# Product-key expert slots worked in chunks of two instead of four, with a head's routing split into five pieces

## What is computed

```python
def peer_ffn(xn, w_query, sub_keys, peer_u, peer_v):
    q = (xt @ w_query).reshape(t, PEER_HEADS, 2, PEER_HALF)
    sk = jnp.einsum('thcd,ckd->thck', q, sub_keys).astype(jnp.float32)
    top_s, top_i = lax.top_k(sk, PEER_TOPK)
    cand_s = top_s[:, :, 0, :, None] + top_s[:, :, 1, None, :]
    ...
    best_s, best_pos = lax.top_k(cand_s, PEER_TOPK)
    idx = jnp.take_along_axis(cand_i, best_pos, axis=-1)
    gate = jax.nn.softmax(best_s, axis=-1)
    ...
        h = jnp.einsum('thkd,td->thk', peer_u[ib], xb).astype(jnp.float32)
        a = (gb * jax.nn.gelu(h, approximate=False)).astype(xb.dtype)
        return jnp.einsum('thk,thkd->td', a, peer_v[ib])
```

## Time and profile before

| | |
|---|---|
| median of 3 runs | 3038.73 us (3035.6 to 3039.03) |
| profiled execution | 3042.86 us, span 3041.1 us |
| busy: PE, DVE, ACT, POOL | 69%, 71%, 37%, 39% of the span |
| share of DMA in the chain that ended last | 37% |
| bytes moved | 1170.89 MB, of which 1073.81 MB are gathers |

### The profile page before, as it was taken

The page is one execution under the profiler, slowest core; times in us unless marked ns, Lnnn a source line. Parts: engine busy times, 40 slices in busy tenths (PEclk is TensorE's granted clock), DMA queues, the critical chain, the costliest instruction groups (busy, mean ns, idle before and its releaser), DMA issues.

```text
span 3041.1 us, 37523 instructions
## 1 busy us (share of the span) xinstructions
PE 2109.0 (69%) x12704; PEld 1048.0 (34%) x12704; DVE 2148.6 (71%) x5267; ACT 1129.8 (37%) x3444; POOL 1191.1 (39%) x1028
## 2 busy tenths in 40 slices
PE   7868688667886877566676777667677556565556
PEld 6654354224442433133343343224344111111111
DVE  4645678887667778777656878887766777776665
ACT  3412345653233444533223445552323322222222
POOL 0014333343443344343444444343444444444443
PEclk9889899778987898788888889878998767767777
DMA  4159999989999999999999999989999999999998
GB/s 158 61 219 418 375 410 414 385 342 414 404 419 406 416 419 419 370 351 419 413 410 420 415 396 420 401 355 392 420 420 421 418 420 419 419 417 419 409 421 357
DMA packets 173840, 1170.89 MB, mean 385 GB/s; under 512 B 19280, under 2 KB 19408, under 8 KB 42576
## 3 DMA queue, kind: packets, MB, share of 16 engines
q0 software_dynamic: 147456, 1073.81, 86.2%
q1 hardware_dynamic: 26192, 94.68, 8.1%
HBM read 1166.32 MB, written 2.10 MB: 384 GB/s over the span
## 4 chain that ended last, share of the span: by engine, by line
DMA 37%; DVE 23%; PE 23%; ACT 8%; issue 6%; POOL 3%; DVEq 0%; SPq 0%; POOLq 0%; ACTq 0%
DMA gather<-experts,idx 37%; PE ysum L548 13%; DVE gather L1039 12%; PE bank L406 5%; POOL gather L364 3%; DVE sd L816 3%; PE bank L507 2%; ACT diag L755 2%; ACT amp L747 2%; ACT L597 1%; ACT gel L740 1%; DVE x L1016 1%; ACT sd L597 1%; DVE shared L843 0%; PE bank L453 0%
## 5 line engine op out<-in xcount | busy, mean ns | idle before, releaser
L364 POOL DMA_INDIRECT gather<-experts,idx x1024 | 1190.9, 1163 | 1830.1 <-PE ysum L548 1492.2
L548 PE MATMUL ysum<-gather,diag 64*64 64x512 f32 x8192 | 1277.6, 777 | 797.3 <-ACT diag L755 751.2
L1039 DVE CUSTOM_DVE_ANT_0 gather<-gather,xc 128x1024 f32<-128x1024 f32 x1024 | 1224.3, 1224 | 585.8 <-DMA gather<-experts,idx 583.5
L548 PEld LDWEIGHTS ysum<-gather,diag 64*64 64x64 f32 x8192 | 369.6, 174 | 1606.4 <-ACT diag L755 966.9
L740 ACT ACTIVATE gel<-hdot 128x4 f32<-128x4 f32 x255 | 52.4, 205 | 1662.9 <-DVE hdot L1039 1662.9
L406 PE MATMUL bank<-xnT,w 128*128 128x256 f32 x1984 | 468.9, 392 | 11.8 <-DVE xnT L805 11.8
L406 PEld LDWEIGHTS bank<-xnT,w 128*128 128x128 f32 x1984 | 378.3, 195 | 108.8 <-issue 45.3
L755 ACT ACTIVATE diag<-cc,amp 128x64 f32<-128x64 f32 x1020 | 268.5, 333 | 2.2 <-PE ysum L548 2.2
L747 ACT ACTIVATE amp<-gel,gate 128x1 f32<-128x1 f32 x1020 | 216.8, 283 | 8.3
L816 DVE RECIPROCAL sd<-sd 128x256 f32<-128x256 f32 x60 | 105.1, 1751 | 119.5 <-ACT sd L597 119.3
L740 ACT ACT_TABLE_LOAD x124 | 159.1, 1283 | 2.2
(11 more groups left out here) (116 smaller groups left out, 1497.6 us busy)
## 6 DMA issues: line engine op xcount, KB each, us to landing
w<-weights SPq DMA_DIRECT2D x168, 512.0 KB, 8.0
gather<-experts,idx POOLq DMA_INDIRECT x1024, 11.8
y_out<-x SPq DMA_DIRECT2D x4, 512.0 KB, 7.7
x<-x_in SPq DMA_DIRECT2D x2, 512.0 KB, 5.4
g2b<-g_rows SPq DMA_DIRECT2D x2, 512.0 KB, 11.2
x<-x_in SPq DMA_DIRECT2D x1, 1024.0 KB, 12.1
cc<-consts_in SPq DMA_DIRECT2D x1, 635.5 KB, 6.6
late<-late_in SPq DMA_DIRECT2D x2, 256.0 KB, 9.0
```

Of the source, the lines that this page charges most:

```text
L364: pool.indirect_dma_start(gather[:, n % SLOTS, :], None, uv_d[m // 2], bass.IndirectOffsetOnAxis(ap=idx[:, g % 2, k:k + 1], axis=0)).then_ ...
L548: mm = nc.tensor.matmul(ysum[outs, q * 512:(q + 1) * 512], diag[toks, n % NDIAG, :], gather[toks, n % SLOTS, DM + hf * 512:DM + (hf + 1) * ...
L1039: e = V.tensor_tensor_reduce(out=gather[:, n % SLOTS, 0:DM], in0=gather[:, n % SLOTS, 0:DM], in1=xc[:, :], scale=1.0, scalar=0.0, op0=ALU. ...
```

## The change

`CH` goes from 4 to 2, so a head now has eight chunks (`PH = TOPK // CH`) and a block has 128 chunks rather than 64. Everything counted in chunks follows: a GELU covers two columns, DVE signals after two dots, DVE may begin a chunk when the GELU two chunks back (so two slots further on) is done, and `interleave` has 128 places to put the same 71 slices. A head's routing is cut into five pieces: the first key search after chunk 0, the second with the 256 sums after chunk 1, the top-16 of the sums after chunk 2, the new function `route_index` after chunk 3, the gate after chunk 6. ACT's `gate_exp` moves behind chunk 2. A wait of DVE for its own last dot stands before `xc` is overwritten at a tile's start. In the first head of block 0 both key searches stand behind chunk 1.

```diff
-CH = 4
+CH = 2
+PH = TOPK // CH
...
-                g = m * TT * HEADS + c // 4 + 1
-                if c % 4 == 1 and g < NBLK * TT * HEADS:
+                g = m * TT * HEADS + c // PH + 1
+                if c % PH == 2 and g < NBLK * TT * HEADS:
                     gate_exp(act, g)
...
-        def route_keys(dve, m, head):
+        def route_keys(dve, m, head, c):
 
             t, h = divmod(head, HEADS)
             done(dve, m, ("sk", t, h))
-            for c in range(2):
-                top16(dve, scores[:, t, 2 * h + c, :], sc2[:, c, :], top_v[:, c, :], top_i[:, c, :])
+            top16(dve, scores[:, t, 2 * h + c, :], sc2[:, c, :], top_v[:, c, :], top_i[:, c, :])
+            if c == 0:
+                return
...
             V.tensor_scalar(neg_best[:, :], best_v[:, 0:1], -1.0, None, ALU.mult).then_inc(s_gm, 1)
+
+        def route_index(dve, m, head):
+
+            g = m * TT * HEADS + head
             V.tensor_scalar(pos_u[:, 0, :], best_p[:, :], 4, None, ALU.logical_shift_right)
...
+                    if cg:
+
+                        dve.wait_ge(s_h, cg)
                     chain(dve, V.scalar_tensor_tensor(xc[:, :], x[:, t, :], r2[:, t:t + 1], g2b[:, :],
                                                       ALU.mult, ALU.mult))
...
-                    if c % 4 == 0:
-                        route_keys(dve, nm, nh)
-                    elif c % 4 == 1:
+                    if c % PH < 2:
+
+                        for half in ((c % PH,) if cg > 1 else () if cg == 0 else (0, 1)):
+                            route_keys(dve, nm, nh, half)
+                    elif c % PH == 2:
                         route_experts(dve, nm, nh)
-                    elif c % 4 == 3:
+                    elif c % PH == 3:
+                        route_index(dve, nm, nh)
+                    elif c % PH == 6:
                         route_gate(dve, nm, nh)
```

More of the change, by code:

```diff
@@ L724, in last_diagonals @@
             for j in range(CH):
-                n, k = c * CH + j, c % 4 * CH + j
+                n, k = c * CH + j, c % PH * CH + j
                 act.wait_ge(s_hlast, j + 1)
@@ L730, in last_diagonals @@
                 nc.scalar.activation(amp[:, c % 2, j:j + 1], gel[:, c % 2, j:j + 1], ACT.Copy,
-                                     scale=gate[:, c // 4 % 2, k:k + 1]).then_inc(s_a, 1)
+                                     scale=gate[:, c // PH % 2, k:k + 1]).then_inc(s_a, 1)
                 act.wait_ge(s_a, n + 1)
@@ L741, in diagonals @@
             act.wait_ge(s_gl, c + 1)
-            if c % 4 == 0:
-                act.wait_ge(s_gate, c // 4 + 1)
+            if c % PH == 0:
+                act.wait_ge(s_gate, c // PH + 1)
             for j in range(CH):
-                k = c % 4 * CH + j
+                k = c % PH * CH + j
                 nc.scalar.activation(amp[:, c % 2, j:j + 1], gel[:, c % 2, j:j + 1], ACT.Copy,
-                                     scale=gate[:, c // 4 % 2, k:k + 1]).then_inc(s_a, 1)
+                                     scale=gate[:, c // PH % 2, k:k + 1]).then_inc(s_a, 1)
             for j in range(CH):
@@ L1023, in peer_dve @@
                 t = (m % 2) * TT + c // per_tile
-                head = c // 4
+                head = c // PH
                 if c % per_tile == 0:
@@ L1086, in _ @@
             first = head_start(mixer, 3)
-            route_keys(dve, 0, 0)
+            route_keys(dve, 0, 0, 0)
+            route_keys(dve, 0, 0, 1)
             route_experts(dve, 0, 0)
+            route_index(dve, 0, 0)
             route_gate(dve, 0, 0)
```

## The result

The changed kernel takes 3125.05 us (median of 4 runs, 3123.84 to 3125.53), the kernel before 3038.88 us beside it: a ratio of 1.0283 (95% interval 1.0267 to 1.0299), 86 us slower. The forecast was 3012 us.

A forecast was written before the change was run, and what follows sets the result against it. Slots were taken to be bound by DMA, with 94 us lost in dips of its rate as the ceiling. Gains of 18 + 4 + 5 = 27 us gave a median of about 3012 us, range 2982 to 3035.

The forecast's parts named there:

- the three DVE stretches: Three 80 us mixer stretches, DVE mostly busy, losing 43.4 us: shorter waits for the square root give net 4 us back.
- The terms that were summed: Gains of 18 us in six queueing stretches, 4 in three stretches with DVE mostly busy, 5 in small dips.
- The hole at 363 to 376 us: Queueing stretch where PE waits 8.0 us for a projection's input: 6 of its 7.6 us should come back.
- ACT's added work: More GELUs (52 us) and table loads (29.5 us) on ACT, costed at nothing because ACT has idle time.
- The slower one: Rival, chance 0.08: with less routing ahead, reciprocals in three DVE-busy stretches wait longer for the root; 22 us slower, about 3061.
- The clock case: Rival, chance 0.12: halved runs of PE slot matmuls lower the granted clock, costing 22 us; net 5 us gained, 3034.

The follow-up runs named there:

- second experiment: Changed kernel, but PE alone runs each mixer slice one chunk (two slots) earlier than DVE and ACT do: 3013.05 us, 0.9922 of the kernel before.
- the grid of four: Changed kernel with slices behind every second chunk on DVE and ACT, ahead of every second on PE: 3010.96 us, 0.9914 of before.
- third experiment: Changed kernel with chunks of two, but a head's routing in whole pieces behind the same slots as before: 3141.84 us, 1.0346 of before.

## Why the prediction was wrong

**The step that failed** is the one on the three DVE stretches and on what a chunk covers: "DVE's work is the same ... What can shrink is the wait for the square root", 4 us back. I counted what ACT does between a chunk's last dot and the root (0.95 us less) and what routing stands ahead of the reciprocal (0.4 us charged), and left out where PE starts. PE's part of a slice had been hidden by a whole chunk's dots. Halving the chunk took half of that cover, 2.4 us, from every slice that has a part on PE. The waits that hang on it, root, scores and output projection on DVE, grew by 75 + 81 + 19 = 175 us. Giving the lead back (second experiment) took 112 us off the time; against the kernel before the loss is 86, because chunks of two by themselves gain 26. I had read the order of PE, and its own excerpt in the section on the change shows the projection between chunks of two; I read it only for what it did for one hole.

**The terms that were summed did hold, where the lead is kept.** With it restored in either way the kernel takes 3011 to 3013 us, the forecast 3012, and the mixer stage runs at 407 to 408 GB/s, the forecast "about 407". So the 27 us were right as a sum, but part of that is luck, since the terms behind it did not come in as priced. The hole at 363 to 376 us, 6 us of the 27, is gone in the changed kernel (no dip in its 340 to 380 us, 419 GB/s), but 380 to 460 us there run at 339 and 332 GB/s, where they had 415 and 406. With the grid of four the hole stays (335 GB/s), and the same gain lies elsewhere. With whole routing and a lead of two (third experiment) it is gone too (420 GB/s), so it was PE's order that closed it and not the half of `route_experts`. ACT's added work left no loss that shows, as the prediction had it: 1242 and 1235 us busy in these two kernels, 112 and 105 us more than before, where some 80 were named. Two readings were slightly off without changing the forecast: the earlier trace rows has nine slices below 401 GB/s behind the third, not ten, and one of the clocks of the earlier trace rows is 0.80, not "0.79 and below".

**The rivals.** The slower one had the right sign, and the wait it watches did grow: over all 60 reciprocals of the span the mean wait for the root is now 194.0/60 = 3.2 us (before 119.3/60 = 2.0), where it had set 2.9 for the 17 of the three stretches. Its mechanism did not make this loss: with the lead of two, keeping the routing whole left that wait as it was (196.3 us). With a lead of four whole routing did shorten it, from 107.9 to 74.7 us, but the time stayed the same. The clock case did not come: 0.86 before and after in the mixer stage, and 0.76 against 0.72 without a mixer. The Trainium skill, page "Perfetto Trace Analysis", section "Matmul Optimizations", says that matmuls should run back to back in batches because the engine's power follows its use. Here batches of slot matmuls half as long did not lower the mean clock of either stage; in the poor stretches it is 0.78 to 0.83, where those of the earlier trace rows had 0.76 to 0.80.

**The lead in one row.** No slot: 3388 us (chunks of four). Two slots: 3125. Four slots: 3013, 3011 on the grid (both chunks of two), and 3036 to 3039 with chunks of four. Six slots: 3049. Too short, and DVE and ACT wait for PE inside slices; too long, and PE waits for them with the slot matmuls behind it. What stays open is whether each stage of the mixer has its own best lead, which wasn't tried.

## What to carry to other kernels

Where two streams of work are woven together on in-order engines, the chunk of one is the cover of the other: before it is made smaller, ask which producer's start is set by it, and keep the distance between producer and consumer in time, not in chunks. Smaller chunks and finer places for the other stream's pieces are two changes, and here only the first was worth having: 26 us with the places left on the old grid (3011 us), and no more with the finer ones (3013 us). A wait of an idle engine is worth following one engine further than the one that it names: DVE waited for ACT, ACT for PE, and PE had only been started late.

## What was not expected of the hardware

Nothing of the chip itself. What surprised was how steep the lead is: 2 slots of it, 2.4 us of dots, cost 112 us over a mixer stage of some 2200 us with no engine over 75% busy, and two slots too many cost 36 us.
